# Retrieval kernel, u stage: another order of four row loads, and every third low part on GpSimd

## The reference

```python
def block(xb):
    q = (xb @ wq).reshape(nb, PEER_HEADS, 2, PEER_DKEY // 2)
    s = jnp.einsum('nhpd,hpkd->nhpk', q, sub_keys).astype(jnp.float32)
    sv, si = lax.top_k(s, PEER_TOPK)
    cand = (sv[:, :, 0, :, None] + sv[:, :, 1, None, :]).reshape(nb, PEER_HEADS, PEER_TOPK * PEER_TOPK)
    ...
    fv, fi = lax.top_k(cand, PEER_TOPK)
    eidx = jnp.take_along_axis(cidx, fi, axis=-1)
    g = jax.nn.softmax(fv, axis=-1)
    u = expert_u[eidx]
    vv = expert_v[eidx]
    act = jax.nn.gelu(jnp.einsum('nhkd,nd->nhk', u, xb).astype(jnp.float32), approximate=False)
    return jnp.einsum('nhk,nhkd->nd', (g * act).astype(xb.dtype), vv)
```

## Time and profile before

| | |
|---|---|
| median of three runs | 2079.47 us (2079.33 to 2083.72) |
| the profiled execution's own time | 2076.02 us |
| its span, first to last instruction | 2074.3 us |
| u stage, first to last product | 696.8 to 1459 us |
| expert stage and end | 1459 to 2074 us |
| PE busy | 1920.2 us (93%) |
| DVE busy | 1345.8 us (65%) |
| POOL busy | 926.8 us (45%) |
| ACT busy | 891.6 us (43%) |
| moved by DMA | 447.33 MB, mean 216 GB/s |

### The profile page before, as it was taken

How to read it: one execution, slowest core, us unless ns; L and a number is a source line. 1 busy time by engine, 2 the same in 40 slices (tenths; PEclk the granted TensorE clock), 3 DMA queues, 4 the chain that set the end, 5 groups by cost and what they waited for, 6 DMA issues and landing times. The chain is left out here.

```text
span 2074.3 us, 32412 instructions
## 1 busy us (share of the span) xinstructions
PE 1920.2 (93%) x11569; PEld 1821.8 (88%) x11569; DVE 1345.8 (65%) x2561; ACT 891.6 (43%) x1936; POOL 926.8 (45%) x831
## 2 busy tenths in 40 slices
PE   7999979997887997989999999998799999999997
PEld 6978768886887997989999999998799999999996
DVE  2134623435423599999989967664387877777775
ACT  4031112334213333637877888875233333333333
POOL 4433313231212354628989999996022222222210
PEclk9999989998997998999999999999899999999999
DMA  7611172226216367898989999999599999999982
GB/s 171 123 52 52 37 176 81 79 68 209 93 30 124 89 180 192 262 246 247 263 254 259 286 263 296 294 275 285 190 322 350 330 351 337 345 346 333 352 304 82
DMA packets 312284, 447.33 MB, mean 216 GB/s; under 512 B 35996, under 2 KB 248476, under 8 KB 308796
## 3 DMA queue, kind: packets, MB, share of 16 engines
q1 hardware_dynamic: 275260, 311.02, 50.1%
q0 software_dynamic: 36864, 134.23, 20.7%
HBM read 375.79 MB, written 68.23 MB: 214 GB/s over the span
## 5 line engine op out<-in xcount | busy, mean ns | idle before, releaser
L1337 PE MATMUL ps<-x_high,uT_high 128*128 128x416 f32 x1024 | 376.3, 367 | 31.8 <-DVE uT_low L1324 21.5
L1594 POOL TENSOR_SCALAR area<-iota_row,chosen 128x128 f32<-128x128 f32 x416 | 371.7, 906 | 3.1
L1937 PE MATMUL ps<-hid_high,v_high 128*128 128x416 f32 x1024 | 359.9, 351 | 12.4 <-DVE hid_low L1910 12.4
L1337 PE MATMUL ps<-x_high,uT_low 128*128 128x416 f32 x1024 | 366.5, 358 | 0.0
L1337 PE MATMUL ps<-x_low,uT_high 128*128 128x416 f32 x1024 | 364.4, 356 | 0.0
L1937 PE MATMUL ps<-hid_low,v_high 128*128 128x416 f32 x1024 | 359.6, 351 | 0.0
L1937 PE MATMUL ps<-hid_high,v_low 128*128 128x416 f32 x1024 | 359.5, 351 | 0.0
L1232 POOL DMA_INDIRECT gathered_rows<-in_peer_v_dram,gathered_index x128 | 135.3, 1057 | 438.4 <-DVE gathered_acc L1269 349.4
L1881 ACT CAST v_high<-area 128x1024 fp32r<-128x1024 f32 x128 | 134.3, 1049 | 390.4 <-PE ps L1937 386.4
L1908 DVE TENSOR_TENSOR v_low<-area,v_high 128x1024 fp32r<-128x1024 f32 x128 | 156.8, 1225 | 134.8 <-ACT v_high L1881 134.8
L1337 PEld LDWEIGHTS ps<-x_high,uT_high 128*128 128x128 f32 x1024 | 197.3, 193 | 40.3 <-DVE uT_low L1324 25.3
(11 more groups left out here) (288 smaller groups left out, 3822.2 us busy)
## 6 DMA issues: line engine op xcount, KB each, us to landing
u_nat<-in_peer_u_dram SPq DMA_DIRECT2D x512, 128.0 KB
area<-in_peer_v_dram SPq DMA_DIRECT2D x128, 512.0 KB
hidden<-gelu_out SPq DMA_DIRECT2D x128, 208.0 KB
routing<-dense SPq DMA_DIRECT2D x26, 1024.0 KB
area<-hidden SPq DMA_DIRECT2D x120, 208.0 KB
w_raw<-in_w_in_dram SPq DMA_DIRECT2D x44, 512.0 KB, 4.1
routing_in<-routing SPq DMA_DIRECT2D x16, 448.0 KB
area<-routing SPq DMA_DIRECT2D x14, 448.0 KB
```

Of the source, the lines that this page charges most:

```text
L1337: ins = self.nc.tensor.matmul(self.k.ps[:, b, 0:N], w[:, b, kk, :], x[:, kk, 0:N], start=(kk == 0 and p == 0), stop=(kk == KD - 1 and p == 2))
L1594: ins = nc.gpsimd.tensor_scalar(first[:, b % AREAS, f, :], iota[:, :], chosen[:, 0, c:c + 1], None, ALU.is_equal)
L1937: ins = nc.tensor.matmul(ps[:, kk, 0:N], v[:, b, kk * P:(kk + 1) * P], h[:, b, :], start=(n == 0 and p == 0), stop=(n == P - 1 and p == 2))
```

## The change

Two things change. The four loads of a tile are issued in the order of quarters 0, 2, 1, 3 in place of 0, 1, 2, 3. And POOL goes on making low parts after the first batch of routing: those of the tiles whose number can be divided by three, 21 to 126; DVE makes the rest. `lent` becomes a list, and `low_ready` counts the tiles of it up to n, on POOL's semaphore or, taken off, on DVE's.

```diff
-        self.lent = (0, 0)
+        self.lent = ()
...
     def load(self, sp, n):
         v = n % USLOTS
         after(sp, self.turned, n - USLOTS + 1)
-        for a in range(QUARTERS):
+        for a in (0, 2, 1, 3):
             sp.dma_start(self.u_nat[a * BLK:(a + 1) * BLK, v, :].rearrange("i (g d) -> i g d", g=P // BLK),
                          self.peer_u[0, n * P:(n + 1) * P, a * D // QUARTERS:(a + 1) * D // QUARTERS].rearrange("(g i) d -> i g d", i=BLK)
                          ).then_inc(self.u_loaded[v], 16)
...
     def on_pool(self, n):
-        return self.lent[0] <= n < self.lent[1]
+        return n in self.lent
 
     def low_ready(self, eng, n):
 
-        first, end = self.lent
+        lent = sum(m <= n for m in self.lent)
         if self.on_pool(n):
-            eng.wait_ge(self.k.pool_low_done, PH + n - first + 1)
+            eng.wait_ge(self.k.pool_low_done, PH + lent)
         else:
-            eng.wait_ge(self.low_done, n + 1 - (end - first if n >= end else 0))
+            eng.wait_ge(self.low_done, n + 1 - lent)
...
     plan = Plan()
-    hidden.lent = (2, min(plan.routing))
+    calm = min(plan.routing)
+    hidden.lent = [n for n in range(2, P) if n < calm or n % 3 == 0]
```

## The result

The changed kernel takes 2114.99 us (median of four runs, 2112.02 to 2127.36) against 2081.59 us for the kernel before in the same comparison, 33 us more. The profiled execution took 2112.02 us (span 2110.3), 36.0 more than that of before. The forecast was 2105 with a range of 2074 to 2136.

The account below looks back on a forecast made before the run. POOL, beside PE, was taken to bound products 53 to 122, DVE products 21 to 42. The terms 26.2 + 2.8 - 3.6 gave +25.4 us, 2101.4 for the profiled execution; adding 3.45 forecast 2105 us, range 2074 to 2136.

Parts of the forecast that it names:

- The bound, and the sign: Products 53 to 122: POOL, beside PE, sets the end of these steps, so more POOL work makes the kernel slower.
- The long stretch, +26.2: Products 53 to 122: 24 low parts at net 1.49 us (2.37 less 0.88 relief), less 9.6 slack: 26.2 us longer.
- Steps 43 to 52, +2.8: Three more POOL low parts at net 1.49 us, less 1.7 us of waits for dots: 2.8 us longer.
- Steps up to 42, -3.6: Products 21 to 42: DVE loses 9.5 us of work, its dots held up by POOL lose 5.9: 3.6 us shorter.
- The bound of +9.4: Products 21 to 42, worst case: each dot waits out a whole POOL low part, 9.4 us longer.
- Tile 126, 0: Last five products: POOL is idle when it makes this low part, so no change in time.
- The order of the quarters, 0: The u loads in the new order: same bytes through the same engines, so 0, with bounds of -7.7 and +7.7 us.
- the gain to which the earlier trace were read to lean: Tail: alternating port sets shortens u loads, so DVE's wait goes, a gain of 7.7 us.
- DVE's relief: Rival, long stretch: fewer DVE low parts bring POOL's one-hots below 736 ns; faster, about 2066 us; chance 0.10.
- The order shortened no loads: Denies the rival that the new order shortens loads and the tail's 7.7 us go: 2072 us; chance 0.06.
- Nothing was absorbed: Denies the rival that POOL's cost is absorbed, all low ends holding at once: no change, 2081 us; chance 0.09.
- PE's clock did fall: Rival, POOL's full stretches: waits lower PE's clock at 27 low parts, 46 us more: 2151 us; chance 0.10.

Follow-up runs that it names:

- POOL's work taken out elsewhere: Changed kernel with old load order; from step 53, where POOL makes a low part, DVE makes the first batch's one-hots: 2086.50 us, ratio 1.0021.
- POOL relieved in the kernel before: Two runs on the kernel before: DVE makes second-batch one-hots (2063.49 us, 0.9926); DVE's low parts from tile 44 read one SBUF input (2062.00 us, 0.9903).
- the run with one input: Kernel before, but from tile 44 DVE's low part reads zeros from PSUM and one SBUF input, in two halves: 2062.00 us, ratio 0.9903.
- every second tile: Kernel before, with POOL also making low parts of every second tile from 54 on, old load order: 2128.14 us, ratio 1.0233.
- early tiles alone: Kernel before, with POOL also making low parts of tiles 21, 24, ... 42 only, old load order: 2082.45 us, ratio 1.0014.
- order alone: Kernel before with only the order of the four u loads changed to 0, 2, 1, 3: 2084.02 us, ratio 1.0009.
- the second run of the changed kernel: Changed kernel unedited, run again beside its version with the old load order: 2117.35 us, ratio 1.0175.
- the one-input form on POOL: Kernel before, with POOL also taking tiles 21, 24, ... 42, computing high x 0 from tile 21 on, old load order: 2079.74 us, ratio 0.9990.

## Why the prediction was right, and where not

**The bound, and the sign.** Right. The reading that POOL, not DVE, sets the end of steps 53 to 122 is borne out from both sides: POOL's work taken out elsewhere removes the loss (1.0021 in place of 1.0211), POOL relieved in the kernel before makes it faster (0.9926, 0.9903).

**The long stretch, +26.2.** The right mechanism, mis-sized: it became 31.8 us longer. By its own working: 24 x 2.42 = 58.1 of new work for 24 x 2.37 = 56.9; relief of 13.0 + 2.7 = 15.7 us, or 0.65 for each tile, in place of 24 x 0.88 = 21.1; and idle time of POOL down by 9.6 us (26.6 to 17.0, span less busy), 8.7 of it from the two waits that were counted as slack. 58.1 - 15.7 - 9.6 = 32.8 is bookkeeping, as busy and idle time make up the stretch; the 1 us that it is off is work at the borders. So the relief was the term that was too large. The four other profiles with 24 low parts there bear this out: at equal counts of one-hots and gather issues, the five give 11 to 20 us of relief, 0.64 for each tile in the mean. But the slack is not so firm. In those four POOL was idle for 20.6 to 30.7 us, and the stretch was 453.4 to 458.0 us long, so that 31.8 is the lowest of five differences from the 416.1 of before; the highest is 41.8. The rate of 0.92 for a DVE low part that no longer stops POOL is right (the run with one input); but the new low part on POOL makes DVE's dots longer (1258 to 1452 ns, and 1716 ns with every second tile). That these longer dots hold POOL up in turn would explain the missing 0.23 us a tile; that was not tried, and the cause stays open.

**Steps 43 to 52, +2.8.** 3.5 us measured. Right, as far as single profiles can tell: five profiles with these low parts show 64.5 to 67.7 us for these products, six with the same work there but without them 60.0 to 64.1.

**Steps up to 42, -3.6.** This step failed: products 0 to 42 became 7.0 us longer. Six profiles with these low parts on POOL show 249.9 to 255.0 us for the first 43 products (mean 252.0), seven without them 247.9 to 250.3 (mean 248.8): about +3, and the run of the early tiles alone had a ratio of 1.0014. The step "if each new low part meets one dot, 8 x 0.74 = 5.9 us are lost again" was too low: the 26 dots lost 26 x (1.501 - 1.255) = 6.4 us against the 25 of before (31.2 us in the same stretch), and the copy of the sort another 2.2. Together 8.6, more than the 7.9 that DVE was relieved of. The prediction counted dots alone as instructions that POOL can hold up. This explains why nothing was gained, not the rest of the loss. DVE's busy time in products 21 to 42 rose by 5.1 us: beside the 0.7 left over from above, one transpose, one dot and eight maxima of the sort, 4.1 us in all, fall inside the stretch now and did not before. DVE's idle time rose by 3.1 us, nearly all of it ahead of dots (3.6 us, 3.0 of them for gathers, against 0.7). In a step POOL issues the gathers behind its low part; that they came late for this reason was not tried. The prediction let POOL's new work hide in its waits and did not ask what comes behind it. The bound of +9.4 held.

**Tile 126, 0.** Wrong by 4.9 us in the kernel's favour, and not by tile 126 alone: the last five products are shorter (27 to 30 us) in every run in which low parts slow the long stretch, with the new order of loads or without, and 34 to 36 in all others. It was not forecast and its cause was not looked into. The wait of the earlier trace rows there fell from 7.7 to this:

```profile
PE ps L1337 <- DVE uT_low L1324: 2.2, 1, 2.2
```

**The order of the quarters, 0.** Right as far as the order alone goes (1.0009); the gain to which the earlier trace rows were read to lean did not come.

**The rivals.** DVE's relief did not win: it wanted one-hots below 736 ns, and they went to 880. The relief was also less than 0.88 a tile, not more. The order shortened no loads. Nothing was absorbed. PE's clock did fall, 0.98 to 0.96 in the long stretch, and PE was busy 13 us longer there; but in the second run of the changed kernel the clock was 0.98, PE busy for 408.6 us, and the stretch 453.4 us long, not shorter than 447.9. That fits the argument of the prediction that PE's slower products hide in its waits for POOL; two profiles do not show it.

**What was to show it.** 55 and 73 low parts, as foretold; POOL busy for 0.96 of a stretch of 448 us (442 foretold); one-hots 880 ns (850). PE's waits for POOL's low part and one-hots came to 34.4 us, not over 40. DVE's waits before its transposes for POOL's low part: 23.4 us. Products 21 to 42 did not get shorter.

The sum, 25.4 in place of 36.0, is short by 10.6: +5.6 long stretch, +0.7 steps 43 to 52, +10.6 up to 42, -4.9 last five, -1.4 ahead of the first product. The long stretch, whose mechanism was right, is most of the loss. That the total came as near as it did is partly luck: the wrong sign up to step 42 is more than half made up for by the last five products, which the sum had at nothing, and by the start, which it did not have.

## What to carry to other kernels

An engine that is idle for half of the whole execution (POOL was busy for 45% of it) can be the one that sets the pace in a part of it: work is moved to it only after a look at the stretch in which it will land. When two engines hold each other up, the price of a moved instruction is its duration there, less what the other side stops holding up, plus what it newly holds up on the engine that was to be relieved, every copy and dot there included. And the stretch that shows an engine at 94% with waits of the next one behind it also says which way to move work: here from POOL to DVE, a little at a time, until the next wait appears.

## What had not been expected of the hardware

A low part on POOL stretched a one-input copy of 128x128 uint32 on DVE from 0.22 us to 2.42. In four of the five other profiles with these low parts it took 2.40 to 2.42 us as well, and with the one-input form on POOL none took over 0.31. So not only two-input instructions of DVE can be held up by it.

On POOL the form with one SBUF input was not faster than the one with two: 2.77 us at its shortest for 128x1024 (high x 0), against 2.37 for the difference.

One and the same program gave profiles in which the long stretch took 447.9 and 453.4 us; with the same work in that stretch (before, order alone, early tiles alone) it took 416.1, 418.3 and 423.5. A difference of a few microseconds in one stretch of one profile is therefore no finding here.
